# A paged MLA cache loop on one core: absorbed queries as extra columns of the key weights, keys in three banks, rope scores by page pairs

## The chip, the core and the metric

One core of a Trainium2 chip runs the whole kernel. TensorE (matrix products), VectorE, ScalarE and GpSimd each work through their own instructions in order; SyncE issues the DMAs. They wait for each other through semaphores. The metric is the time of one execution in microseconds, as the median of several runs.

## The reference, cut to what matters

The kernel computes one step of a decoder layer for 256 prompt tokens and for 8 sample sequences. The part that matters here is the attention of the samples over their cache. Each of the 8 sequences has 2048 past tokens, in 16 pages of 128; a page row holds a latent of 512 values and a rope key of 64. For each page, in the reference's words:

```python
def mla_keys(latent, w_uk, w_uv, k_norm_nope):
    c, kr = latent[..., :KV_LORA], latent[..., KV_LORA:]
    kn = rms_norm((c @ w_uk).reshape(bsz, s, MLA_HEADS, NOPE_DIM), k_norm_nope)
    v = (c @ w_uv).reshape(bsz, s, MLA_HEADS, V_DIM)
    return kn, kr, v

def mla_scores(qn, qr, kn, kr):
    s = jnp.einsum('bqhd,bkhd->bhqk', qn, kn) + jnp.einsum('bqhr,bkr->bhqk', qr, kr)
    return s.astype(jnp.float32) * MLA_SCALE
```

followed by a softmax over all tokens and a weighted sum of the values. The key of a token is divided by its root mean square in each head, so the full keys (`c @ w_uk`, 1024 columns, 8 heads of 128) have to be made for every cached token, if only for their squares. Beside this run the prompt's own attention, the gated-delta heads, and after the loop gates, merge and an MLP.

## The kernel before

**The loop.** The cache loop goes over `NT` = 128 pages, `n` = 0 to 127, in `NG` = 32 groups of four (`g = n // 4`, `t = n % 4`); one sample has four groups. There is no planner: every engine has its own loop over `n`, written out by hand, and the order in it is the order in which it works. Work of the rest of the layer is woven in as 256 slots, `beside(2 * n)` and `beside(2 * n + 1)`: prompt attention first (`front_pe` and the like), a few decay steps (`decay_steps`), then four pairs of gated-delta heads (`pair_pe`, `pair_act`, `pair_dve`), each of 49 slots.

**A page.** SyncE loads it into `clat` and `crope`, twelve pages at a time in a ring. VectorE separates its 16-bit halves (`split_planes`), a transposing DMA turns them, and ScalarE puts them together as `cTr` (`turned_page`), then rounds to the high part `cTh`. VectorE subtracts (`split_lo`) and gets the low part `cTl`. The key weights are in a high part `ukh` and a low part `ukl` as well, 1024 columns each. TensorE makes the keys in two halves of 512 columns (`keys(n, half_)`), each half in one of the banks 0 to 2 of PSUM, in 12 products: for each of four chunks of the latent `cTh` with `ukh`, `cTh` with `ukl` and `cTl` with `ukh` (lines 2016, 2017 and 2018). The page's latent is the stationary operand, loaded ahead of each product as 128 columns; the weights stream past it. ScalarE squares each half head by head out of PSUM and sums (`squares`, L851), into `kss`. Once a group is full, GpSimd raises its 32 columns to the power -1/2 (`rk`, L705).

**Scores.** The query of a head is folded through the key weights once ("absorbed", `qeff`), so that the scores need no finished keys, only `rk`. `qeff[:, s]` of sample `s` has 16 columns in each of five parts: columns 0 to 7 in parts 0 to 3 are the absorbed query, columns 8 to 15 in part 4 the rope part. Once in a group, at `t == 3`, `query_products` multiplies the latents of four pages (`cTr`, fp32, 512 moving columns, L2037) and the turned rope keys `rpT` (L2040) with it. The four chunks of the latent go to four strips of bank 4 and have to be added later. An fp32 product shows as two records, because it is done in two passes. ScalarE copies the bank to `prows` (`score_rows`, L862), TensorE turns it in four transposes a page later (`score_columns`, L2046), and VectorE adds the four strips (`score_parts`, L1240) to `sparts`. Then `scaled` multiplies by `rk` and adds the rope scores, `maxima` and `exps` make the softmax weights, and `weigh` (L2056) sums the page latents with them, a group and a page later. `rope_columns` (L2027) turns the rope keys of a group at `t == 2`, two pages in one transpose, and ScalarE copies them to `rpT` (`turned_rope`).

**Around it.** Before a bank is written again the key products wait for its squares: `wait(pe, "ksq_ready", k - 2)`, where `k` counts the halves and the bank is `k % 3`. After the last page come the column groups for gates and z (`z_unit`), which use banks 0 to 3.

Of the kernel before, what the change touches and what calls it, by code (L numbers as in the profile page):

```python
# [13 lines left out]
F32 = mybir.dt.float32  # L14
# [171 lines left out]
def build(nc, I, O):  # L186
    C_in, ctx = I["consts"], ExitStack()
    with ctx:
# [35 lines left out]
        qeff, e = place("qeff", [P, NS, 5, 16], F32, taken["rsq"][0])  # L224
# [5 lines left out]
        ukh, o = place("ukh", [P, 4, D], F32R, o)  # L230
        ukl, o = place("ukl", [P, 4, D], F32R, o)
# [97 lines left out]
        sparts, o = place("sparts", [P, 2, 4, 2, H], F32, o)  # L329
# [5 lines left out]
        gate, o = place("gate", [1, 1], F32, o)  # L335
        olat, _ = place("olat", [P, NS, 4, H], F32, taken["prows"][0])
# [123 lines left out]
        B_TR, B_SCORE, B_PAIR, B_ROWS = 3, 4, 5, 7  # L460
        trp = ps[:, B_TR, :].rearrange("p (c n) -> p c n", c=4)
        stp = ps[:, B_SCORE, :].rearrange("p (t n) -> p t n", t=4)

        def sum_bank(gg):

            return ps[:, 3 if gg < NG - 2 else 4, :]

        def latent_bank(s_):
            return sum_bank(4 * s_ + 3).rearrange("p (c n) -> p c n", c=4)

# [15 lines left out]
        def _(sp):  # L486
# [134 lines left out]
            sp.wait_ge(S("half_done"), 2 * NT)  # L621
            sp.wait_ge(S("qk_done"), NG)
# [52 lines left out]
        def _(g):  # L675
# [21 lines left out]
            nc.gpsimd.memset(qeff[:], 0.0).then_inc(S("pool_clear"), 1)  # L697
# [16 lines left out]
        def _(act):  # L714
# [116 lines left out]
            def turned_page(n):  # L831
# [3 lines left out]
                else:  # L835
                    act.wait_ge(S("tr_landed"), 16 * (n - 1))
                    if n % 4 == 0:
                        wait(act, "qk_done", n // 4)
                    nc.scalar.activation(cTr[:, :, tokens(n)].bitcast(U16).rearrange("p c (t x) -> p x c t", x=2), turned[:, n % 2].bitcast(U16).rearrange("p (x c t) -> p x c t", x=2, c=4), ACT.Copy).then_inc(S("ct_raw"), 1)  # L839
                act.wait_ge(S("ct_raw"), n + 1)  # L840
                wait(act, "half_done", 2 * (n - 1))
# [12 lines left out]
            def turned_rope(gg):  # L854
                act.wait_ge(S("rope_done"), gg + 1)
                wait(act, "qk_done", gg)
                nc.scalar.activation(rpT[:], ps[:, B_SCORE, 0:2 * P], ACT.Copy).then_inc(S("rope_ready"), 1)
# [140 lines left out]
            for n in range(NT):  # L998
# [5 lines left out]
                if t == 3:  # L1004
                    score_rows(g)
# [5 lines left out]
                squares(n, 1)  # L1011
            z_high(2)
# [72 lines left out]
        def _(v):  # L1085
# [147 lines left out]
            def split_lo(n):  # L1233
                v.wait_ge(S("ct_hi"), n + 1)
                wait(v, "half_done", 2 * (n - 1))
                V.tensor_tensor(cTl[:, n % 2], cTr[:, :, tokens(n)], cTh[:, n % 2].bitcast(F32), ALU.subtract).then_inc(S("ct_lo"), 1)  # L1236

            def score_parts(gg):
                v.wait_ge(S("st_done"), gg + 1)
                V.tensor_reduce(sparts[:, gg % 2].rearrange("p t a h -> p t (a h)"), stp.rearrange("p t (c n) -> p t n c", c=4)[:, :, 0:16, :], AX, ALU.add).then_inc(S("s_parts"), 1)  # L1240

            def scaled(gg):
                y = gg % 2
                v.wait_ge(S("s_parts"), gg + 1)
                v.wait_ge(S("rk_ready"), gg + 1)
                V.tensor_tensor(ssc[:, y], sparts[:, y, :, 0, :], rk[:, y], ALU.mult).then_inc(S("s_half"), 1)
                v.wait_ge(S("s_half"), gg + 1)
                V.tensor_tensor(ssc[:, y], sparts[:, y, :, 1, :], ssc[:, y], ALU.add).then_inc(S("s_ready"), 1)
# [55 lines left out]
            def front_dve(i):  # L1304
# [19 lines left out]
                if i == 4:  # L1324
                    v.wait_ge(S("pool_clear"), 2)
                    for g in range(2):
                        V.tensor_copy(qeff[:, :, 0:4, 4 * g:4 * g + 4], a_bank(f"qcol{g}").rearrange("p (c q x) -> p x c q", c=4, q=4)[:, 0:NS]).then_inc(S("a_read"), 1)
                    qx = qeff[:, :, 4, 8:16].rearrange("p s (a b) -> p a b s", b=2)
                    v.wait_ge(S("qrs_ready"), 1)
                    V.tensor_copy(qx[0:64, :, 0, :], qr[0:64, :, TP:T])  # L1330
                    V.tensor_copy(qx[64:128, :, 1, :], qr[64:128, :, TP:T])
                    v.wait_ge(S("qr64_landed"), 32)
                    V.tensor_copy(qx[0:64, :, 1, :], qr64[0:64])
                    V.tensor_copy(qx[64:128, :, 0, :], qr64[64:128]).then_inc(S("qeff_ready"), 1)
# [326 lines left out]
            for n in range(NT):  # L1661
# [4 lines left out]
                if t == 0 and g >= 1:  # L1666
                    score_parts(g - 1)
# [7 lines left out]
                if n == NT - 1:  # L1675
                    score_parts(g)
# [5 lines left out]
                if t == 3:  # L1682
                    v.wait_ge(S("ksq_ready"), 2 * n + 2)
# [172 lines left out]
        def _(pe):  # L1856
# [153 lines left out]
            def keys(n, half_):  # L2010
                k, cols = 2 * n + half_, slice(512 * half_, 512 * half_ + 512)
                out = ps[:, k % 3, :]
                pe.wait_ge(S("ct_lo"), n + 1)
                wait(pe, "ksq_ready", k - 2)
                for c in range(4):
# [3 lines left out]
                i.then_inc(S("half_done"), 1)  # L2019
# [513 lines left out]
```

## Time and profile before

| | us |
|---|---|
| median of 3 runs | 1457.36 |
| lowest and highest run | 1457.14, 1457.37 |
| span of the profiled execution (first to last instruction) | 1455.6 |
| TensorE busy | 1445.4 (99%) |
| ScalarE busy | 868.4 (60%) |
| VectorE busy | 808.5 (56%) |
| GpSimd busy | 217.1 (15%) |

The profile is of one execution, and its times count from its first instruction. It gives the span only; the runs are timed as a whole and have what lies around the span in them too. Durations of matrix products overlap, since they are pipelined: the time from one start to the next is what a product takes of the engine. A weight load has records of its own ("PEld"). A timeline joins neighbouring instructions of one line into one row with their number behind an x.

### The profile page before, as it was taken

What the parts mean: (1) busy time and instruction counts of PE and PEld (TensorE: products, weight loads), DVE (VectorE), ACT (ScalarE), POOL (GpSimd) and SP (SyncE); (2) the same over time, 40 slices, a digit from 0 to 9 for tenths busy, and PEclk for the clock granted to TensorE, in tenths of its full rate; (3) what the DMA queues carried; (4) which work ended last, traced back from release to release, by engine and by line L of the source; (5) the groups of instructions that cost most, each with busy time, mean ns of one, the idle gap of its engine ahead of it and who ended that gap; (6) DMA issues with size and microseconds to landing.
All of it is one profiled execution on the core that took longest, in us unless ns stands there. A gap on an engine that the chain in (4) does not pass through costs nothing.

```text
span 1455.6 us, 28542 instructions
## 1 busy us (share of the span) xinstructions
PE 1445.4 (99%) x10052; PEld 1182.0 (81%) x10052; DVE 808.5 (56%) x1664; ACT 868.4 (60%) x2816; POOL 217.1 (15%) x111
## 2 busy tenths in 40 slices
PE   9999999999999999999999999999999999999998
PEld 7877777877777777778777787777778999999998
DVE  5865445555546564555655555645434766777643
ACT  5545678686666686575855667766775353344332
POOL 3001111111122111111221111122122000000000
PEclk9999999999999999999999999999999999999999
DMA  9541315653245534365333453333734465555551
GB/s 280 172 119 30 83 26 117 156 116 70 63 102 123 121 86 86 74 132 125 85 70 82 113 139 70 63 70 73 189 77 152 145 235 183 168 172 191 181 174 59
DMA packets 263720, 173.61 MB, mean 119 GB/s; under 512 B 165464, under 2 KB 212088, under 8 KB 263576
## 3 DMA queue, kind: packets, MB, share of 16 engines
q1 hardware_dynamic: 263266, 171.53, 45.3%
q8 instruction: 78, 1.28, 0.4%
q14 instruction: 58, 0.48, 0.1%
q10 hardware_dynamic: 318, 0.33, 0.1%
HBM read 132.22 MB, written 6.74 MB: 95 GB/s over the span
## 4 chain that ended last, share of the span: by engine, by line
PE 96%; DVE 2%; ACT 0%; DMA 0%; ACTq 0%; issue 0%; POOL 0%; DVEq 0%
PE ps L2016 17%; PE ps L2018 16%; PE ps L2017 16%; PE ps L2453 6%; PE ps L2454 6%; PE ps L2455 6%; PE ps L2056 2%; PE ps L2037 2%; PE ps L2109 2%; PE ps L2401 2%; PE ps L2402 2%; PE ps L2110 2%; PE ps L2403 2%; PE ps L2111 2%; PE ps L1894 2%; PE ps L2046 1%
## 5 line engine op out<-in xcount | busy, mean ns | idle before, releaser
L851 ACT ACTIVATE ksq<-ps 128x128 f32<-128x128 f32 x1024 | 268.1, 277 | 279.5 <-PE ps L2018 278.0
L2016 PE MATMUL ps<-ukh,cTh 128*128 128x512 f32 x1024 | 418.4, 409 | 0.3 <-DVE cTl L1236 0.3
L2018 PE MATMUL ps<-ukh,cTl 128*128 128x512 f32 x1024 | 400.7, 391 | 0.0
L2017 PE MATMUL ps<-ukl,cTh 128*128 128x512 f32 x1024 | 399.9, 391 | 0.0
L705 POOL TENSOR_TENSOR rk<-kss,mhalf 128x32 f32<-128x32 f32 x32 | 180.1, 5628 | 478.0 <-DVE kss L1684 478.0
L2016 PEld LDWEIGHTS ps<-ukh,cTh 128*128 128x128 f32 x1024 | 192.6, 188 | 55.8 <-issue 17.1
L2018 PEld LDWEIGHTS ps<-ukh,cTl 128*128 128x128 f32 x1024 | 192.2, 188 | 42.9
L2017 PEld LDWEIGHTS ps<-ukl,cTh 128*128 128x128 f32 x1024 | 192.8, 188 | 34.0
L851 ACT ACTIVATION_READ_ACCUMULATOR ksq<-ps 128x1 f32 x1024 | 212.2, 207 | 0.0
L839 ACT ACTIVATE cTr<-turned 128x1024 uint16<-128x1024 uint16 x126 | 173.8, 1379 | 10.9 <-PE ps L2040 5.7
L1236 DVE TENSOR_TENSOR cTl<-cTr,cTh 128x512 fp32r<-128x512 f32 x128 | 88.4, 691 | 136.9 <-ACT cTh L842 136.0
L1038 ACT ACTIVATE wh<-wraw 128x2048 fp32r<-128x2048 f32 x44 | 84.3, 1916 | 131.3 <-PE ps L2455 126.8
L1688 DVE TENSOR_TENSOR wl<-wraw,wh 128x2048 fp32r<-128x2048 f32 x44 | 100.8, 2291 | 70.3 <-ACT wh L1038 70.3
L1231 DVE COPY planes<-clat 128x1024 uint16<-128x1024 uint16 x126 | 86.2, 684 | 21.8 <-DMA turned<-planes 14.6
L2453 PE MATMUL ps<-Ah,wh 128*128 128x264 f32 x320 | 91.1, 285 | 0.0
L2454 PE MATMUL ps<-Al,wh 128*128 128x264 f32 x320 | 90.9, 284 | 0.0
L2455 PE MATMUL ps<-Ah,wl 128*128 128x264 f32 x320 | 90.6, 283 | 0.0
L842 ACT ACTIVATE cTh<-cTr 128x512 fp32r<-128x512 f32 x128 | 80.9, 632 | 4.1
L2453 PE MATMUL ps<-Hh,wh 128*128 128x264 f32 x256 | 72.8, 284 | 0.0
L2455 PE MATMUL ps<-Hh,wl 128*128 128x264 f32 x256 | 72.7, 284 | 0.0
L2454 PE MATMUL ps<-Hl,wh 128*128 128x264 f32 x256 | 72.6, 284 | 0.0
L2453 PEld LDWEIGHTS ps<-Ah,wh 128*128 128x128 f32 x320 | 60.2, 188 | 0.0
(514 smaller groups left out, 2590.7 us busy)
## 6 DMA issues: line engine op xcount, KB each, us to landing
clat<-cache_mla SPq DMA_DIRECT2D x128, 256.0 KB, 2.6
wraw<-w_in SPq DMA_DIRECT2D x16, 1024.0 KB, 5.1
wraw<-w_up SPq DMA_DIRECT2D x16, 1024.0 KB, 5.4
wraw<-w_down SPq DMA_DIRECT2D x16, 1024.0 KB, 5.0
braw<-w_in SPq DMA_DIRECT2D x24, 512.0 KB, 4.0
crope<-cache_mla SPq DMA_DIRECT2D x128, 32.0 KB, 2.4
sst<-state_gdn SPq DMA_DIRECT2D x32, 128.0 KB, 3.2
gdn_sample<-sst SPq DMA_DIRECT2D x32, 128.0 KB, 2.0
```

The source lines that it names most:

```text
L705: nc.gpsimd.tensor_tensor(rk[:, y], kss[:, y], mhalf[:], ALU.pow).then_inc(S("rk_ready"), 1)
L839: nc.scalar.activation(cTr[:, :, tokens(n)].bitcast(U16).rearrange("p c (t x) -> p x c t", x=2), turned[:, n % 2].bitcast(U16).rearrange(" ...
L851: i = nc.scalar.activation(ksq[:, P * h:P * h + P], ps[:, k % 3, P * h:P * h + P], ACT.Square, accum_out=kss[:, n // 4 % 2, n % 4, 4 * hal ...
L1231: V.tensor_copy(planes[:].bitcast(U16).rearrange("p (x l) -> p x l", x=2), clat[:, n % RING, :].bitcast(U16).rearrange("p (l x) -> p x l", ...
L1236: V.tensor_tensor(cTl[:, n % 2], cTr[:, :, tokens(n)], cTh[:, n % 2].bitcast(F32), ALU.subtract).then_inc(S("ct_lo"), 1)
L1688: V.tensor_tensor(wl2[:, ns % 2], wraw2[:, (ns - NM) % 4], wh2[:, ns % 2].bitcast(F32), ALU.subtract).then_inc(S("w_lo"), 1)
L2016: mm(out, cTh[:, n % 2, c], ukh[:, c, cols], start=c == 0, stop=False)
L2017: mm(out, cTh[:, n % 2, c], ukl[:, c, cols], start=False, stop=False)
L2018: i = mm(out, cTl[:, n % 2, c], ukh[:, c, cols], start=False, stop=c == 3)
L2453: mm(out, w_hi, mh[:, kc, :], start=first and kc == 0, stop=False)
L2454: mm(out, w_hi, ml[:, kc, :], start=False, stop=False)
L2455: k = mm(out, w_lo, mh[:, kc, :], start=False, stop=last and kc == 3)
```

## The change

The absorbed query of the current sample is stored behind the key weights as columns 1024 to 1031, high part in `ukh`, low part in `ukl`. A page's keys are made in three banks: 384, 384 and 256 + 8 columns, with the same three kinds of product each. The last eight columns of the third bank are then the page's scores before scaling, already turned and summed over the chunks; ScalarE copies them to `sparts`. For every new sample (16 pages) VectorE copies that sample's columns into the weights (`query_slot`). The first four pages come before these columns are there; their scores are made once by `first_scores`. The rope scores of a group are two products with the turned rope keys as stationary operand, a pair of pages each, and 16 moving columns of `qrope`. `query_products`, `score_rows`, `score_columns` and `score_parts` are gone.

```diff
-        qeff, e = place("qeff", [P, NS, 5, 16], F32, taken["rsq"][0])
+        qeff, e = place("qeff", [P, NS, 4, H], F32, taken["rsq"][0])
+        qrope, e = place("qrope", [P, NS, 2 * H], F32, e)
+        qeffh, e = place("qeffh", [P, NS, 4, H], F32R, e)
-        ukh, o = place("ukh", [P, 4, D], F32R, o)
-        ukl, o = place("ukl", [P, 4, D], F32R, o)
+        ukh, o = place("ukh", [P, 4, D + H], F32R, o)
+        ukl, o = place("ukl", [P, 4, D + H], F32R, o)
+        KG = [(slice(0, 384), 0, 3, False), (slice(384, 768), 3, 3, False), (slice(768, 1024), 6, 2, True)]
...
-            def squares(n, half_):
-                k = 2 * n + half_
-                act.wait_ge(S("half_done"), k + 1)
-                if half_ == 0 and n % 4 == 0:
+            def squares(n, j):
+                k, (_, h0, count, scored) = 3 * n + j, KG[j]
+                act.wait_ge(S("group_done"), k + 1)
+                if j == 0 and n % 4 == 0:
                     wait(act, "rk_ready", n // 4 - 1)
+                    wait(act, "s_half", n // 4 - 1)
                 wait(act, "ksq_ready", k)
-                for h in range(4):
-                    i = nc.scalar.activation(ksq[:, P * h:P * h + P], ps[:, k % 3, P * h:P * h + P], ACT.Square, accum_out=kss[:, n // 4 % 2, n % 4, 4 * half_ + h:4 * half_ + h + 1])
+                if scored and n >= 4:
+                    nc.scalar.activation(sparts[:, n // 4 % 2, n % 4, :], ps[:, k % 3, P * count:P * count + H], ACT.Copy)
+                for h in range(count):
+                    i = nc.scalar.activation(ksq[:, P * h:P * h + P], ps[:, k % 3, P * h:P * h + P], ACT.Square, accum_out=kss[:, n // 4 % 2, n % 4, h0 + h:h0 + h + 1])
                 i.then_inc(S("ksq_ready"), 1)
...
-            def score_rows(gg):
-                act.wait_ge(S("qk_done"), gg + 1)
-                wait(act, "st_done", gg)
-                nc.scalar.activation(prows[:], ps[:, B_SCORE, :], ACT.Copy).then_inc(S("ssb_ready"), 1)
...
-                if t == 3:
-                    score_rows(g)
...
                 squares(n, 1)
+                squares(n, 2)
...
-            def score_parts(gg):
-                v.wait_ge(S("st_done"), gg + 1)
-                V.tensor_reduce(sparts[:, gg % 2].rearrange("p t a h -> p t (a h)"), stp.rearrange("p t (c n) -> p t n c", c=4)[:, :, 0:16, :], AX, ALU.add).then_inc(S("s_parts"), 1)
+            def query_slot(s_):
+                wait(v, "group_done", 48 * s_)
+                V.tensor_copy(ukh[:, :, D:D + H], qeffh[:, s_])
+                V.tensor_copy(ukl[:, :, D:D + H], qeffl[:, s_]).then_inc(S("slot_ready"), 1)
...
+                v.wait_ge(S("rope_scored"), gg + 1)
+                V.tensor_tensor(ssc[:, y], rope_scores_of(gg), ssc[:, y], ALU.add).then_inc(S("s_ready"), 1)
...
+                    V.tensor_copy(qeffh[:], qeff[:]).then_inc(S("qeff_ready"), 1)
+                    v.wait_ge(S("qeff_ready"), 1)
+                    V.tensor_tensor(qeffl[:], qeff[:], qeffh[:].bitcast(F32), ALU.subtract).then_inc(S("qeff_split"), 1)
...
                 if n + 1 < NT:
                     split_lo(n + 1)
-                if t == 0 and g >= 1:
-                    score_parts(g - 1)
+                if n and n % 16 == 0:
+                    query_slot(n // 16)
...
-            def keys(n, half_):
...
+            def key_chunks(n, j, chunks):
+                k, (cols, _, count, scored) = 3 * n + j, KG[j]
+                if scored and n >= 4:
+                    cols = slice(cols.start, cols.stop + H)
+                    pe.wait_ge(S("slot_ready"), n // 16 + 1)
+                out = ps[:, k % 3, 0:cols.stop - cols.start]
+                if chunks[0] == 0:
+                    pe.wait_ge(S("ct_lo"), n + 1)
+                    wait(pe, "ksq_ready", k - 2)
+                for c in chunks:
...
-                wait(pe, "s_parts", gg)
+                wait(pe, "s_ready", gg)
...
-            def query_products(gg):
...
-                for c in range(4):
-                    mm(ps[32 * c:32 * c + 16, B_SCORE, :], qeff[:, s, c, :], cTr[:, c, :], start=True, stop=False)
...
+            def rope_scores(gg):
+                pe.wait_ge(S("rope_ready"), gg + 1)
+                pe.wait_ge(S("qeff_ready"), 1)
+                for m in range(2):
+                    out = rope_scores_of(gg)[:, 2 * m:2 * m + 2, :].rearrange("p t h -> p (t h)")
+                    k = mm(out, rpT[:, P * m:P * m + P], qrope[:, gg // 4, :], start=True, stop=True)
+                k.then_inc(S("rope_scored"), 1)
+
+            def first_scores():
+                pe.wait_ge(S("ct_raw"), 4)
+                pe.wait_ge(S("qeff_ready"), 1)
                 for t in range(4):
+                    for c in range(4):
+                        k = mm(ps[:, B_ROPE, 384 + H * t:384 + H * t + H], cTr[:, c, tokens(t)], qeff[:, 0, c, :], start=c == 0, stop=c == 3)
...
                 if t == 3:
-                    query_products(g)
+                    rope_scores(g)
+                if n == 3:
+                    first_scores()
...
-                if t == 0 and g >= 1:
-                    score_columns(g - 1)
...
                 beside(2 * n)
-                keys(n, 0)
+                key_chunks(n, 0, (0, 1, 2, 3))
+                key_chunks(n, 1, (0,))
...
                 beside(2 * n + 1)
-                keys(n, 1)
+                key_chunks(n, 1, (1, 2, 3))
+                key_chunks(n, 2, (0, 1, 2, 3))
```

`group_done` counts the three groups of a page where `half_done` counted two halves, and every wait on it is scaled to that. The last two groups' weighing uses bank 7 instead of bank 4, and `z_unit` goes through the banks in the order 3, 0, 1, 2 instead of 3, 1, 2, 0.

## Rows read from the trace of the kernel before

**Rows 1.** Busy time by stretch: the cache loop (us, busy us and instructions of each engine, clock, DMA).
```profile
101.00:1112.80 1011.80, 1011.34 (x6592) 765.37 (x6593) 526.07 (x1386) 681.50 (x2632) 195.60 (x93) 1.00 0.42 94
```

**Rows 2.** Waits in the cache loop, TensorE and ScalarE (us in total, times, longest).
```profile
PE ps L2016 <- DVE cTl L1236: 0.3, 1, 0.3
...
ACT ksq L851 <- PE ps L2018: 276.1, 193, 3.4
```

**Rows 3.** Groups by form, ScalarE: table loads (xcount, busy us, mean ns).
```profile
L870 ACT ACT_TABLE_LOAD x10 | 12.8, 1283 | 0.2
```

**Rows 4.** Timeline of TensorE (start us, duration): 512 columns, quiet and behind other work.
```profile
242.12 0.39 PE L2016 MATMUL ps<-ukh,cTh 128*128 128x512 f32 x1
...
244.62 0.39 PE L2018 MATMUL ps<-ukh,cTl 128*128 128x512 f32 x1
...
710.10 0.40 PE L2017 MATMUL ps<-ukl,cTh 128*128 128x512 f32 x1
...
712.41 0.39 PE L2018 MATMUL ps<-ukh,cTl 128*128 128x512 f32 x1
```

**Rows 5.** Timeline of TensorE: first and last of 36 products of 264 columns.
```profile
1249.73 0.28 PE L2453 MATMUL ps<-Bh,wh 128*128 128x264 f32 x1
...
1253.98 0.29 PE L2455 MATMUL ps<-Bh,wl 128*128 128x264 f32 x1
```

**Rows 6.** Timeline of TensorE's weight loads in that stretch.
```profile
1249.85 0.19 PEld L2455 LDWEIGHTS ps<-Bh,wl 128*128 128x128 f32 x1
1249.97 0.19 PEld L2453 LDWEIGHTS ps<-Bh,wh 128*128 128x128 f32 x1
```

**Rows 7.** Timeline of TensorE around query blocks, alone and before others.
```profile
231.72 0.39 PE L2018 MATMUL ps<-ukh,cTl 128*128 128x512 f32 x1
...
233.35 0.50 PE L2016 MATMUL ps<-ukh,cTh 128*128 128x512 f32 x1
...
555.50 0.39 PE L2018 MATMUL ps<-ukh,cTl 128*128 128x512 f32 x1
...
557.52 0.50 PE L2016 MATMUL ps<-ukh,cTh 128*128 128x512 f32 x1
...
352.24 0.39 PE L2018 MATMUL ps<-ukh,cTl 128*128 128x512 f32 x1
...
352.94 0.50 PE L2016 MATMUL ps<-ukh,cTh 128*128 128x512 f32 x1
```

**Rows 8.** Timeline of TensorE around the score transposes.
```profile
238.72 0.40 PE L2018 MATMUL ps<-ukh,cTl 128*128 128x512 f32 x1
...
239.32 0.48 PE L2016 MATMUL ps<-ukh,cTh 128*128 128x512 f32 x1
239.63 0.39 PE L2017 MATMUL ps<-ukl,cTh 128*128 128x512 f32 x1
```

**Rows 9.** Timeline of TensorE around eight records with 8 columns.
```profile
103.95 0.95 PE L2282 MATMUL ps<-qr,consts_sb 128*128 128x8 f32 x8
104.76 0.48 PE L2016 MATMUL ps<-ukh,cTh 128*128 128x512 f32 x1
```

**Rows 10.** Timeline of ScalarE on pages 15 and 16.
```profile
235.49 0.58 ACT L862 ACTIVATE prows<-ps 128x512 f32<-128x512 f32 x1
...
242.38 0.25 ACT L851 ACTIVATE ksq<-ps 128x128 f32<-128x128 f32 x1
...
243.38 1.34 ACT L839 ACTIVATE cTr<-turned 128x1024 uint16<-128x1024 uint16 x1
```

**Rows 11.** Timelines of VectorE and TensorE on page 48.
```profile
505.69 0.68 DVE L1236 TENSOR_TENSOR cTl<-cTr,cTh 128x512 fp32r<-128x512 f32 x1
...
506.09 0.50 PE L2016 MATMUL ps<-ukh,cTh 128*128 128x512 f32 x1
```

**Rows 12.** Timelines of VectorE and TensorE at page 17.
```profile
245.41 0.69 DVE L1236 TENSOR_TENSOR cTl<-cTr,cTh 128x512 fp32r<-128x512 f32 x1 [1.73 <-ACT cTh L842]
...
246.19 0.50 PE L2016 MATMUL ps<-ukh,cTh 128*128 128x512 f32 x1
```

More of the change, by code:

```diff
@@ L328, in build @@
         prows, o = place("prows", [P, 512], F32, o)
-        sparts, o = place("sparts", [P, 2, 4, 2, H], F32, o)
+        sparts, o = place("sparts", [P, 2, 4, H], F32, o)
         lacc, o = place("lacc", [P, 512], F32, o)
@@ L335, in build @@
         gate, o = place("gate", [1, 1], F32, o)
+        qeffl, _ = place("qeffl", [P, NS, 4, H], F32R, taken["prows"][0])
         olat, _ = place("olat", [P, NS, 4, H], F32, taken["prows"][0])
@@ L855, in turned_rope @@
                 act.wait_ge(S("rope_done"), gg + 1)
-                wait(act, "qk_done", gg)
-                nc.scalar.activation(rpT[:], ps[:, B_SCORE, 0:2 * P], ACT.Copy).then_inc(S("rope_ready"), 1)
-            def score_rows(gg):
-                act.wait_ge(S("qk_done"), gg + 1)
-                wait(act, "st_done", gg)
-                nc.scalar.activation(prows[:], ps[:, B_SCORE, :], ACT.Copy).then_inc(S("ssb_ready"), 1)
+                wait(act, "rope_scored", gg)
+                nc.scalar.activation(rpT[:], ps[:, B_ROPE, 0:2 * P], ACT.Copy).then_inc(S("rope_ready"), 1)
             def exps(gg):
@@ L1234, in split_lo, with first_parts @@
                 v.wait_ge(S("ct_hi"), n + 1)
[L1235 removed]
+                wait(v, "group_done", 3 * (n - 1))
                 V.tensor_tensor(cTl[:, n % 2], cTr[:, :, tokens(n)], cTh[:, n % 2].bitcast(F32), ALU.subtract).then_inc(S("ct_lo"), 1)
[L1238 to L1240 removed]
+            def first_parts():
+                v.wait_ge(S("first_scores"), 1)
+                V.tensor_copy(sparts[:, 0], ps[:, B_ROPE, 384:416].rearrange("p (t h) -> p t h", h=H)).then_inc(S("first_parts"), 1)
+            def query_slot(s_):
+                wait(v, "group_done", 48 * s_)
+                V.tensor_copy(ukh[:, :, D:D + H], qeffh[:, s_])
+                V.tensor_copy(ukl[:, :, D:D + H], qeffl[:, s_]).then_inc(S("slot_ready"), 1)
             def scaled(gg):
                 y = gg % 2
[L1244 removed]
+                if gg == 0:
+                    v.wait_ge(S("first_parts"), 1)
                 v.wait_ge(S("rk_ready"), gg + 1)
[L1246 removed]
+                V.tensor_tensor(ssc[:, y], sparts[:, y], rk[:, y], ALU.mult).then_inc(S("s_half"), 1)
                 v.wait_ge(S("s_half"), gg + 1)
[L1248 removed]
+                v.wait_ge(S("rope_scored"), gg + 1)
+                V.tensor_tensor(ssc[:, y], rope_scores_of(gg), ssc[:, y], ALU.add).then_inc(S("s_ready"), 1)
             def maxima(gg):
@@ L2018, in keys @@
                     i = mm(out, cTl[:, n % 2, c], ukh[:, c, cols], start=False, stop=c == 3)
-                i.then_inc(S("half_done"), 1)
+                if chunks[-1] == 3:
+                    i.then_inc(S("group_done"), 1)
             def rope_columns(gg):
@@ L2023, in rope_columns @@
                     pe.wait_ge(S(f"page_landed{u % RING}"), 32 * (u // RING) + 32)
-                wait(pe, "s_parts", gg)
+                wait(pe, "s_ready", gg)
                 for m in range(2):
                     u = (4 * gg + 2 * m) % RING
-                    k = nc.tensor.transpose(ps[:, B_SCORE, P * m:P * m + P], crope[:, u:u + 2, :].rearrange("p u n -> p (u n)"), ident)
+                    k = nc.tensor.transpose(ps[:, B_ROPE, P * m:P * m + P], crope[:, u:u + 2, :].rearrange("p u n -> p (u n)"), ident)
                 k.then_inc(S("rope_done"), 1)
-            def query_products(gg):
-                s = gg // 4
-                pe.wait_ge(S("ct_raw"), 4 * gg + 4)
+            def rope_scores(gg):
                 pe.wait_ge(S("rope_ready"), gg + 1)
                 pe.wait_ge(S("qeff_ready"), 1)
-                wait(pe, "s_parts", gg)
-                for c in range(4):
-                    mm(ps[32 * c:32 * c + 16, B_SCORE, :], qeff[:, s, c, :], cTr[:, c, :], start=True, stop=False)
-                for t in range(4):
-                    r = slice(64 * (t % 2), 64 * (t % 2) + 64)
-                    k = mm(ps[32 * t:32 * t + 16, B_SCORE, P * t:P * t + P], qeff[r, s, 4, :], rpT[r, P * (t // 2):P * (t // 2) + P], start=False, stop=True)
-                k.then_inc(S("qk_done"), 1)
-            def score_columns(gg):
-                pe.wait_ge(S("ssb_ready"), gg + 1)
-                for t in range(4):
-                    k = nc.tensor.transpose(stp[:, t, :], prows[:, P * t:P * t + P], ident)
-                k.then_inc(S("st_done"), 1)
+                for m in range(2):
[5 more added lines that the diff above has]
+                pe.wait_ge(S("qeff_ready"), 1)
+                for t in range(4):
+                    for c in range(4):
+                        k = mm(ps[:, B_ROPE, 384 + H * t:384 + H * t + H], cTr[:, c, tokens(t)], qeff[:, 0, c, :], start=c == 0, stop=c == 3)
+                k.then_inc(S("first_scores"), 1)
             def weigh(gg):
@@ L2390, in z_unit @@
                 pe.wait_ge(S("w_lo"), ns + 1)
-                for j in ((3, 1, 2, 0) if i == 0 else range(4)):
+                for j in ((3, 0, 1, 2) if i == 0 else range(4)):
                     if i == 0 and j == 3:
@@ L2394, in z_unit @@
                     elif i == 0:
-                        pe.wait_ge(S("ksq_ready"), max(k + 1 for k in range(2 * NT) if k % 3 == j))
+                        pe.wait_ge(S("ksq_ready"), 3 * (NT - 1) + j + 1)
                     if i >= 2 and i % 2 == 0:
```

47 lines of the change are left out of this document (22 added, 25 removed).

## The prediction

> **What bounds the kernel now.** I read the stretches first. The cache loop runs from 101 to 1112.8 us, 1011.8 of the 1455.6 us; TensorE is busy for 1011.34 of it at a granted clock of 1.00, which is the 2.4 GHz level, while VectorE has 526 us of work and ScalarE 682 [rows 1]. Busy time of a pipelined engine proves little, so I read the waits next: in the loop the key products wait once, for 0.3 us, and ScalarE spends 276 us waiting for them [rows 2]. So TensorE's instruction stream sets the pace in every part of the loop, and an edit is worth what it adds to that stream or takes from it, until another engine comes late. The third view is therefore the timeline of TensorE, read from start to start, because durations overlap there: a 512-column product lasts 0.39 us but the next starts after 0.23.
>
> Start to start: in a quiet stretch 11 products of 512 columns take 2.50 us, 0.227 each; behind other work 10 take 2.31 us, 0.231 [rows 4]. I use 0.229. Products of 264 columns: 35 steps in 4.25 us, 0.1214 each [rows 5]. At 2.4 GHz the columns alone are 0.2133 and 0.1100 us, so a product costs its columns and a further 0.0157 us (512) or 0.0114 us (264).
>
> **Part 1: keys in three banks.** A page had 24 products of 512 columns; it gets 24 of 384 and 12 of 264 (256 on the first four pages). No row has 384 columns. Its bounds are columns plus the one or the other surcharge, 0.1714 and 0.1757; between two measured sizes I take the middle, 0.1736. Then a page costs 24 x 0.1736 + 12 x 0.1214 = 5.62 us against 24 x 0.229 = 5.50: +0.127 us, times 128 = **+16.3 us**. With the small surcharge throughout it is +9.6, with the large one in all 36 products +29.4. These are the ends.
>
> The Trainium skill ("TensorE: Matmul & The Clock Gate", Back-to-back issue gap) gives a warm product columns / 2.4 GHz and about 2.5 ns. By that rule the estimate for this part would be 9 us instead of 16. The trace does not agree at either size (0.227 and 0.1214 us where the rule has 0.216 and 0.1125), so the rows decide.
>
> **Part 2: query products go, rope scores come.** Alone in its place, the block of old query and rope products stretches the way from the last key product to the next from 0.23 to 1.63 us: 1.40. In front of a block of small products the way is 2.02 us, with that block alone 0.70: 1.32 [rows 7]. There are 32 blocks, one for each group of four pages. The new rope scores are two fp32 products, four records, each behind a load of 128 columns. The nearest row is eight records of this kind with 8 moving columns: 0.81 us from their start to the next key product's, 0.10 to 0.11 each [rows 9]. Four add 0.37 alone and 0.45 before others. Eight groups stand alone and save 1.03, 24 save 0.87: **-29.1 us**, with ends -28 and -33. The first key behind such a block has a longer step (0.34 instead of 0.23) before and after the change; it stays.
>
> **Part 3: score transposes go.** Four a group: the way is 0.60 us instead of 0.23, and the next step 0.31 instead of 0.23 [rows 8], together 0.45; 0.44 where others follow. 32 times: **-14.1 us**.
>
> **Part 4: the first page group.** 16 products with loads of 128 columns and 8 moving columns, in two passes 32 records at 0.11 [rows 9]: **+3.6 us**, once, on TensorE's own stream. The transposes of rope stay as they are.
>
> **Part 5: the other engines.** ScalarE loses 32 row copies of 0.58 us, 18.6 us, and gains 124 copies of 8 columns, each at most the 0.25 of a square over 128 columns [rows 10], so at most 31 us. VectorE loses a reduction a group and gains two small copies for each of eight samples, and at the front a split of the query columns. GpSimd's power step gets its sums somewhat earlier, and the sum with the rope scores is read a page before the next rope transposes want that bank. All of it is covered by the 330 us and 486 us in which these engines have nothing to do in the loop [rows 1]; without that cover it would be at most some 10 us. After the last key product of a page ScalarE has now one small copy and two squares to make instead of four before it turns the next page, about 0.3 us less. So the next page's operands come a little earlier.
>
> **Part 6: new waits.** There are now as many groups a page as banks, so each page needs the same bank again: from a group's end to its reuse some 3.5 us of key products, where it was 5.5. And the third group of every 16th page waits for VectorE to put in the new query columns, which stands in its queue behind the split of the next page. Seven such pages. On six it is covered; the latest split is on page 48: it ends at 506.37 and with the two copies, some 0.2 us each, at about 506.8, while the second half of the keys starts at 506.09 [rows 11], and the third group starts 1.4 us behind that point (24 products of 384 columns before it instead of 12 of 512), at 507.5. On page 16 it isn't covered. There ScalarE goes through several table loads (decays, exponentials): the squares of page 15's second half start only at 242.38, and page 17 is turned from 243.38 on [rows 10], split at 245.41, and page 17's keys start at 246.19, with nothing to spare [rows 12]. In the new order: without the row copy (0.58), with one square fewer ahead (0.25) and 0.35 from page 14, the squares start at about 241.2 and are done at 242. The keys of page 15 and 16 come 1.3 us earlier (the two blocks above), so page 16 begins at 238.05 and wants bank 1 at 240.1: it waits 2.0 us. The second group ends at 244.2; the split, 0.6 earlier than before, ends at 245.4, the two copies at 245.9: another 1.7 us. Queued behind that waiting product are the rest of page 16, the weighing of page values and page 17; nothing after them makes it up. **+3.7 us**, from 0 to 6. Page 116, where a late transposing DMA leaves small room, adds **0.3**.
>
> **Sum.** +16.3 - 29.1 - 14.1 + 3.6 + 3.7 + 0.3 = -19.3 us. The profiled span is 1455.6; the median of the runs is 1457.36, 1.8 us more for what lies around the span and does not change. 1457.4 - 19.3 = **1438 us**. Of 1457 us, 0.2% is 2.9 us, about what a measurement of this kernel can tell from no change.
>
> **Rivals.**
> *The surcharge does not shrink with the columns* (0.0157 in all 36). For it: it is larger in the 512-column rows behind other work. Against it: 0.0114 at 264. 1438 + 13 = 1451 us. Chance 0.12.
> *The surcharge is the small one, and page 16 waits less.* 1438 - 6.7 - 3.7 = about 1428 us. Chance 0.12.
> *Banks come free late, slower than before.* The mechanism: a table load of ScalarE (1.28 us) ahead of squares holds a bank that the next page now needs 2 us sooner. The loop has some 26 such places besides page 16, ten before exponentials [rows 3] and, by the code, four each for silu, exp and two roots. If each held TensorE for its 1.28 us, it would cost 33 us: 1471. It outweighs the gain from 0.74 us a place. Against it: ScalarE waits for key products 193 times in the loop [rows 2], so it is mostly early; page 16 has three table loads in 6 us, the others one or two. Chance 0.08.
> *Weight loads become the bound.* A page has 36 loads instead of 24, each 0.19 us. If no product could follow sooner than a load takes, a page would need 36 x 0.188 = 6.8 us, +146 us over the forecast: 1584. Against it: in the later stages loads of 0.19 us start every 0.12 us [rows 6], so they overlap. Chance 0.01.
> The Trainium skill ("Perfetto Trace Analysis", Identifying the Most-Contended Engine) asks to judge TensorE by the busy share of its loads, which speaks against this change: it rises. Here the stretch with 264 columns has loads without a gap [rows 6] and still runs at columns plus 0.011 us, so the share names no bound.
> *The change frees nothing.* Another chain (pages by DMA, turning, splitting) is just as long as TensorE's, and what is saved comes back as waits: 1457. Against it: 276 us of ScalarE's waiting. Chance 0.05.
> The forecast keeps 0.62, with its own range 1431 to 1446.
>
> **Chances and range.** Both surcharge cases end faster than 1454.4, so faster has 0.62 + 0.12 + 0.12 = 0.86, and 0.01 of the last rival's milder forms: 0.87. Same 0.05. Slower 0.08 (the 1471 and the load bound, less that 0.01). The range takes in the forecast and most of the two surcharge cases: 1430 to 1450.
>
> **What would show it.** Key products of 384 columns starting every 0.172 to 0.175 us, of 264 every 0.121 to 0.123; no records with 16-column weights over 512 moving columns, nor of the score transposes; four records of rope scores a group within 0.45 us; 32 short records once near 124 us. Near page 16 TensorE standing still twice, for some 2 us each, behind squares and behind the copies into the key weights. The loop shorter by 19 us, the rest after it unchanged. It is wrong if the step of 384 columns is above 0.18, or if waits for squares show in many pages.

## The result and the profile after

The changed kernel takes 1442.04 us (median of 4 runs, 1440.28 to 1442.27) against 1457.36; the ratio is 0.9888, 95% interval 0.9877 to 0.9900. That is 15.3 us less where 19.3 were forecast, inside the stated range. The profiled execution has a span of 1440.5 us. The stretches first, loop and rest (columns as in [rows 1]):

```profile
102.90:1098.20 995.30, 992.02 (x7650) 923.31 (x7651) 517.59 (x1372) 686.30 (x2727) 197.99 (x93) 1.00 0.43 96
1098.20:1440.50 342.30, 338.19 (x2817) 334.57 (x2816) 214.28 (x203) 132.43 (x107) 6.12 (x3) 1.00 0.52 170
```

From the first key product to the last it is 995.1 us, before 1011.8 [rows 1]: 16.7 less. The rest after the loop is the same within 0.2. The stage ahead of the loop, which the change hardly touches, took 1.8 us more in this profile; more on that below. TensorE has 1058 more records in the loop and still sets the pace; its loads now show 923 us of 995, and no wait in the loop names a load.

The waits in the loop, for TensorE and for ScalarE (us in total, times, longest):

```profile
PE ps L2035 <- ACT ksq L859: 1.5, 1, 1.5
PE ps L2035 <- DVE ukl L1247: 1.2, 1, 1.2
PE ps L2100 <- DVE qkv L1511: 0.5, 1, 0.5
PE ps L2035 <- DVE cTl L1238: 0.3, 1, 0.3
```

```profile
ACT ksq L859 <- PE ps L2037: 182.4, 157, 3.0
```

The first two lines are the two waits that the prediction put on page 16, each once in 128 pages. ScalarE still waits far more for TensorE than the other way round. The timeline of TensorE shows where they lie (L2035 to L2037 are the three kinds of key product):

```profile
244.65 0.34 PE L2037 MATMUL ps<-ukh,cTl 128*128 128x384 f32 x1
246.45 0.41 PE L2035 MATMUL ps<-ukh,cTh 128*128 128x384 f32 x1 [1.47 <-ACT ksq L859]
...
248.46 0.34 PE L2037 MATMUL ps<-ukh,cTl 128*128 128x384 f32 x1
249.97 0.39 PE L2035 MATMUL ps<-ukh,cTh 128*128 128x264 f32 x1 [1.16 <-DVE ukl L1247]
```

Page 16's second group stands for page 15's squares, its third for the query columns of the second sample.

Now the step of the new widths, on page 124, where little other work runs. First rows of the two widths and the last of the page:

```profile
1077.60 0.34 PE L2037 MATMUL ps<-ukh,cTl 128*128 128x384 f32 x1
...
1079.13 0.28 PE L2037 MATMUL ps<-ukh,cTl 128*128 128x264 f32 x1
```

From 1077.60, the last of 384 columns, there are 12 steps to 1079.13. The first of them is the step of a 384-column product, the other eleven are of 264 columns: 1.53 - 0.175 = 1.35, 0.123 each. Over the whole loop, record to record, without waits and without the few steps in which the clock was at its lower level (below), 2749 steps of 384 columns inside a run of key products have a mean of 0.1754 us and 1372 steps of 264 have 0.1216; the 2622 steps of 512 before had 0.2289. With the steps at the lower clock in it the mean for 384 is 0.1758, so such means of two kernels can be compared only when both leave them out. The prediction took 0.1736, 0.1214 and 0.229.

The rope scores and the first scores, in the same timeline:

```profile
126.34 0.52 PE L2055 MATMUL ps<-qrope,rpT 128*128 128x16 f32 x4
126.70 3.72 PE L2063 MATMUL ps<-qeff,cTr 128*128 128x8 f32 x32
130.28 1.10 PE L2324 MATMUL ps<-qr,consts_sb 128*128 128x256 f32 x2
130.82 0.88 PE L2035 MATMUL ps<-ukh,cTh 128*128 128x384 f32 x1
131.50 0.52 PE L2036 MATMUL ps<-ukl,cTh 128*128 128x384 f32 x1
```

The block of 32 short records takes 3.6 us, as forecast. The products behind it were not forecast: 0.52 us long instead of 0.34 and 0.32 from start to start instead of 0.175. The stretches there show why (the third number from the end is the granted clock):

```profile
126.00:130.00 4.00, 4.00 (x39) 4.00 (x37) 0.00 (x0) 0.63 (x5) 0.00 (x0) 1.00 0.28 53
130.00:134.00 4.00, 4.00 (x16) 3.82 (x16) 1.82 (x4) 2.00 (x2) 0.00 (x0) 0.57 0.00 0
134.00:138.00 4.00, 4.00 (x27) 3.95 (x26) 1.79 (x4) 1.66 (x12) 0.00 (x0) 1.00 0.00 0
```

The clock is at its lower level, 1.2 GHz, for 3.4 us right behind the block, although TensorE was never idle in it.

The loop's balance, in the prediction's parts (sums of steps from start to start over all records of the loop):

| | forecast | measured |
|---|---|---|
| keys, steps and seams | +16.3 | +21.1 (754.1 - 730.3 - 2.7 of waits) |
| query products against rope scores | -29.1 | -29.6 (42.3 to 12.6) |
| score transposes | -14.1 | -13.4 |
| first scores | +3.6 | +3.6 |
| waits on page 16 | +3.7 | +2.7 |
| page 116, others | +0.3 | -1.1 |
| loop | -19.3 | -16.7 |

The lower clock is inside these numbers, mostly in the keys' row; an experiment prices it at 1.6.

### The profile page after: what moved, and what is told of

Its sections match the earlier page's. It is cut to its first block, busy times and chain, and to the rows that moved or that the text cites. A ratio compares the mean times of both kernels' runs of the same rounds, so it can differ in the third digit from the quotient of the medians.

```text
span 1440.5 us, 30928 instructions
## 1 busy us (share of the span) xinstructions
PE 1427.6 (99%) x11108; PEld 1340.9 (93%) x11108; DVE 800.0 (56%) x1651; ACT 872.6 (61%) x2908; POOL 219.4 (15%) x111
## 4 chain that ended last, share of the span: by engine, by line
PE 95%; ACT 2%; DVE 2%; issue 0%; POOL 0%; DVEq 0%; ACTq 0%
PE ps L2035 17%; PE ps L2036 16%; PE ps L2037 16%; PE ps L2470 6%; PE ps L2471 6%; PE ps L2472 6%; PE ps L2073 2%; PE ps L2126 2%; PE ps L2418 2%; PE ps L2419 2%; PE ps L2127 2%; PE ps L2420 2%; PE ps L2128 2%; PE ps L1909 1%; PE ps L2055 1%; PE ps L2100 1%
## 5 line engine op out<-in xcount | busy, mean ns | idle before, releaser
L2035 PE MATMUL ps<-ukh,cTh 128*128 128x384 f32 (+1 forms) x1536 | 507.4, 330 | 2.9 <-ACT ksq L859 1.5
L2036 PE MATMUL ps<-ukl,cTh 128*128 128x384 f32 (+1 forms) x1536 | 491.9, 320 | 0.0
L2037 PE MATMUL ps<-ukh,cTl 128*128 128x384 f32 (+1 forms) x1536 | 491.4, 320 | 0.0
L2035 PEld LDWEIGHTS ps<-ukh,cTh 128*128 128x128 f32 x1536 | 289.8, 189 | 24.3 <-issue 17.6
L2036 PEld LDWEIGHTS ps<-ukl,cTh 128*128 128x128 f32 x1536 | 289.5, 188 | 0.8
L2037 PEld LDWEIGHTS ps<-ukh,cTl 128*128 128x128 f32 x1536 | 288.9, 188 | 0.0
L859 ACT ACTIVATION_READ_ACCUMULATOR ksq<-ps 128x1 f32 x1024 | 209.2, 204 | 0.0
L2471 PEld LDWEIGHTS ps<-Al,wh 128*128 128x128 f32 x320 | 60.2, 188 | 0.0
```

The costliest lines, as they stand in the source:

```text
L2035: mm(out, cTh[:, n % 2, c], ukh[:, c, cols], start=c == 0, stop=False)
L2036: mm(out, cTh[:, n % 2, c], ukl[:, c, cols], start=False, stop=False)
L2037: i = mm(out, cTl[:, n % 2, c], ukh[:, c, cols], start=False, stop=c == 3)
L2471: mm(out, w_hi, ml[:, kc, :], start=False, stop=False)
```

## The experiments

All comparisons of a few us are made by the length of the loop, first to last key product, in the profiles. Steps are means over the loop at the upper clock, without waits. Two profiles of the unaltered changed kernel gave 995.13 and 995.14 us. The medians of the runs move by 2 us with the stage ahead of it.

### Three banks alone

The kernel before, with nothing of the change but the three groups of key columns:

```diff
...
+        KG = [(slice(0, 384), 0, 3), (slice(384, 768), 3, 3), (slice(768, 1024), 6, 2)]
...
-                keys(n, 0)
+                key_chunks(n, 0, (0, 1, 2, 3))
+                key_chunks(n, 1, (0,))
...
-                keys(n, 1)
+                key_chunks(n, 1, (1, 2, 3))
+                key_chunks(n, 2, (0, 1, 2, 3))
...
```

> The kernel before with one part of the change alone: keys in banks of 384, 384 and 256 columns, no score columns; query products and score transposes stay. Theory (the three banks cost 24 x 0.1758 + 12 x 0.118 - 24 x 0.2289 = 0.14 us a page, 18 us in all, some 3 less at the seams, and a wait for squares on page 16 of 1 to 3 us): 1457.4 + 17 = 1474 us, from 1472 to 1478. Rival (reusing each bank on every page makes waits in many pages): above 1485, with waits of key products for squares in many pages. Rival (the banks cost what the surcharge of 0.0136 said): 1457.4 + 11 = 1468.

1473.74 us (ratio to before 1.0110, 1.0093 to 1.0127), the loop 1027.9, 16.1 more than before. Its waits:

```profile
PE ps L2019 <- ACT ksq L852: 1.4, 1, 1.4
PE ps L2019 <- DVE cTl L1238: 0.3, 1, 0.3
```

So the reuse of a bank on every page costs one wait of 1.4 us, not one in many pages. The other 14.7 us are the smaller products, and both rivals are out. One number did not fit: its 384-column steps have a mean of 0.1744 us, where the changed kernel has 0.1754.

### The first scores in four parts

```diff
...
-                if n == 3:
-                    first_scores()
+                if n in (3, 4):
+                    first_scores(2 * (n - 3))
...
+                if n in (3, 4):
+                    first_scores(2 * (n - 3) + 1)
                 beside(2 * n + 1)
...
```

(the parts left out make one score block of one page per call and fit the waits on it)

> The changed kernel with the 32 records of the first scores not in one block, but eight at a time between four blocks of key products (pages 3 and 4). Theory (the block of 32 records with 8 moving columns is what the clock falls behind, to the lower level for 3.4 us, which costs about 1.9 us): no fall between 120 and 145 us in the profile, 1442.0 - 1.9 = 1440.1 us. Rival (the fall comes at any place, as the one at 52 us does where the change has no part): a fall in the loop still, or the time unchanged at 1442.

1438.61 us, the loop 993.5: 1.6 less. The stretch that had the fall, in this kernel:

```profile
124.00:128.00 4.00, 4.00 (x27) 3.95 (x27) 1.87 (x4) 2.77 (x8) 0.00 (x0) 1.00 0.10 19
128.00:132.00 4.00, 4.00 (x30) 3.95 (x29) 1.79 (x4) 1.45 (x12) 0.00 (x0) 1.00 0.00 0
```

The same 32 records, eight at a time between key products, and the clock stays up. In the three kernels with the parts spread, this one and the two joined ones, no profile has a fall in the loop. Nor have the profiles of the kernel before and of the three banks alone, which make no first scores. In all eight profiles of kernels with the block in one piece there is one, and it begins between 127.8 and 130.9 us, from within the block's last records to 1.3 us behind it. The theory holds and the rival doesn't. What it is in the block that brings the fall was not taken apart.

### Query columns ahead of the split

```diff
...
+                if n and n % 16 == 0:
+                    query_slot(n // 16)
                 if n + 1 < NT:
                     split_lo(n + 1)
-                if n and n % 16 == 0:
-                    query_slot(n // 16)
```

> The changed kernel with VectorE putting in the next sample's query columns ahead of the split of the next page instead of behind it. Theory (the second wait on page 16, 1.2 us, is for the place in VectorE's queue): this wait is gone and the time is 1442.0 - 1.2 = 1440.8 us. Rival (page 17 is late anyway, since ScalarE turns it late): the wait moves to page 17's first product, time unchanged.

1440.14 us, the loop 993.7: 1.4 less. The wait for `ukl` is gone and no other came in its place. It was the place in VectorE's queue: two copies of 0.17 us each stood behind a split that waits for ScalarE.

### The sigmoid a page later as well

```diff
-                if i == 2:
+                if i == 4:
                     act.wait_ge(S("rw_clear"), 1)
```

(and the order of the run before)

> The changed kernel with the query columns put in ahead of the split (as in the run before) and the decays' sigmoid, with its table load, moved one page later on ScalarE. Theory (the first wait on page 16, 1.5 us, is for squares that stand behind three table loads in 6 us): that wait is gone too, the loop 993.7 - 1.5 = 992.2 us. Rival (the work is only pushed to page 17, where ScalarE is the later for it): a wait of about the same length on page 17 or 18, the loop unchanged at 993.7.

1440.32 us, the loop 993.3. The wait for squares is gone, but the rival was right:

```profile
PE ps L2378 <- issue: 1.3, 1, 1.3
```

L2378 is the transpose of the decays on page 17, which needs the sigmoid. The wait went from 1.5 to 1.3 us and otherwise only changed its name.

### The same columns as 512, 256 and 264

```diff
-        KG = [(slice(0, 384), 0, 3, False), (slice(384, 768), 3, 3, False), (slice(768, 1024), 6, 2, True)]
+        KG = [(slice(0, 512), 0, 4, False), (slice(512, 768), 4, 2, False), (slice(768, 1024), 6, 2, True)]
...
```

> The changed kernel with the same 1032 columns and the same 36 products a page, split as 512, 256 and 264. Theory (the surcharge over the columns is 0.0156 us for 512 and 384 and 0.008 to 0.012 for 256 and 264, so the loss of part 1 is the width 384): a page costs 12 x (0.2289 + 0.1179 + 0.1217) = 5.62 instead of 5.68 us, 128 pages 7.5 us less: 1434.5 us. Rival (the surcharge is one per product, whatever the width): 1442. Rival (four squares hold the first bank longer than three and the key products wait for it): 256-column steps as in the theory, but waits for squares in several pages and a time of 1438 or more.

1439.85 us, the loop 993.2, 1.9 less; the forecast of 7.5 was wrong. 256 and 264 columns have their steps (0.1186, 0.1211), but 512 columns now take 0.2303 where they took 0.2289 in the kernel before. By these steps a page is 5.64 us against 5.67, 3.8 us in 128 pages. So it isn't the width 384. Here too the wide steps became longer than in the kernel before, and in both kernels the rows of the key weights lie 1032 columns apart instead of 1024. The rest of the difference is a second fall of the clock, 3.4 us long, at 248 us behind the two waits on page 16; at the 1.6 us that the other fall cost it hides nearly half of the gain. The waits are two and 2.7 us in all, as in the changed kernel, so the rival of the four squares is out too.

### The distance of the rows

Only the memory that the key weights take is changed. With it everything placed behind them moves:

```diff
-        ukh, o = place("ukh", [P, 4, D + H], F32R, o)
-        ukl, o = place("ukl", [P, 4, D + H], F32R, o)
+        ukh, o = place("ukh", [P, 4, 1088], F32R, o)
+        ukl, o = place("ukl", [P, 4, 1088], F32R, o)
```

> The changed kernel with the rows of the key weights 1088 columns apart in memory (4352 bytes, a multiple of 256) instead of 1032 (4128 bytes, a multiple of 32); nothing else differs. Theory (the 384-column steps are 0.1758 here and 0.1744 with rows of 1024 columns because of the distance of the rows): steps of 0.1744, 24 x 0.0014 x 128 = 4.3 us less. Rival (the steps are longer because of what the other engines do at that time): steps unchanged at 0.1758, time unchanged.

1436.78 us (ratio to before 0.9847), the loop 990.1: **5.0 us less**, with every wait where it was. Page 124 in this kernel:

```profile
1072.01 0.33 PE L2036 MATMUL ps<-ukl,cTh 128*128 128x384 f32 x1
...
1073.56 0.28 PE L2036 MATMUL ps<-ukl,cTh 128*128 128x264 f32 x1
```

The row at 1072.01 is the second last product of 384 columns, the one at 1073.56 the second last of 264. Between them are 12 steps in 1.55 us. Two of them are steps of 384 columns, together 0.35; the ten of 264 columns share 1.20, 0.120 each. Over the loop the means are 0.1743 for 384 and 0.1199 for 264, against 0.1754 and 0.1216. That is some 3 us in the steps of 384 columns and 2 in those of 264. The expected 4.3 us came from the wide steps alone, at 0.0014 each, a difference that had some of the lower clock in it; they gained 0.0011, and the steps of 264 columns, which the expectation left out, made up for it. The step that it named, 0.1744, is right, and the rival is out.

> As the run with 1088 columns, with rows 1040 columns apart (4160 bytes, a multiple of 64 and not of 128). If the row distance matters by multiples of 64 bytes, steps of 384 columns are 0.1744; if it takes a larger power of two, 0.1758 as with 1032.

1439.24 us (two runs), the loop 994.9. The steps of 384 columns are 0.1751, those of 264 columns 0.1208: both lie between the two other distances, 384 columns nearer to the bad one. The loop hides it, because the fall of the clock lasts twice as long in this profile, 6.8 us:

```profile
126.00:128.00 2.00, 2.00 (x19) 2.00 (x19) 0.00 (x0) 0.00 (x0) 0.00 (x0) 0.95 0.03 8
128.00:130.00 2.00, 2.00 (x9) 1.89 (x9) 0.00 (x0) 0.68 (x1) 0.00 (x0) 0.50 0.00 0
132.00:134.00 2.00, 2.00 (x8) 2.00 (x8) 0.13 (x1) 0.00 (x0) 0.00 (x0) 0.50 0.00 0
```

With the second half of the fall taken off at another 1.6 us, an estimate from the run with the first scores spread, the loop would be 993.3: 1.8 us less than with 1032, where 1088 gives 5.0. So neither branch of the expectation fits: a distance of 4160 bytes, a multiple of 64 and not of 128, is a little better than 4128 and not good. 4096 and 4352, multiples of 256, are. Whether 128 would do was not tried.

At 4160 bytes `ukl` and all that lies behind it start at the same place within 256 bytes as at 4096 and 4352; at 4128 `ukl` alone starts 128 bytes off. So where a tensor starts within 256 bytes does not explain the slow steps at 4160, and the distance of the rows is left. That the tensors also lie at other addresses altogether was not varied by itself.

### Four groups a page

The same as 256, 256, 256 and 264 columns, 48 products a page:

```diff
...
+        KG = [(slice(0, 256), 0, 2, False), (slice(256, 512), 2, 2, False), (slice(512, 768), 4, 2, False), (slice(768, 1024), 6, 2, True)]
...
+                key_chunks(n, 1, (0, 1, 2, 3))
...
+                key_chunks(n, 3, (0, 1, 2, 3))
...
```

> The changed kernel with the 1032 columns in four groups a page: 256, 256, 256 and 264, so 48 products instead of 36. Theory (a product's surcharge grows with its width, 0.012 at 256, 0.0154 at 384): steps of 0.1185 us, a page 36 x 0.1185 + 12 x 0.1217 = 5.73 us, only 0.05 more than with 36 products, 6 us in all, besides waits for banks, since three banks serve four groups. Rival (the surcharge is one for every product that adds): 12 x 0.0154 = 0.18 us a page more, 24 us. Rival (weight loads become the bound): steps of 256 columns well above 0.12 us.

1454.30 us, the loop 1008.4, 13.2 more. Its waits for squares:

```profile
PE ps L2036 <- ACT ksq L859: 7.6, 10, 1.5
```

The waits for squares are 6.1 us more than in the changed kernel, the wait for `ukl` (1.2) is gone, and the products themselves add some 8: 12 more on each of 128 pages, at steps of 0.1185 us for 256 columns. The theory had this step right and 6 us for the products. The rival's 24 is out, and so are the weight loads as a bound at this width. Four groups over three banks show what a bank that comes free late looks like: ten waits instead of one.

### Joined, and the changed kernel once more

```diff
...
-                if t == 3 and g >= 1:
-                    exps(g - 1)
                 beside(2 * n + 1)
                 squares(n, 1)
                 squares(n, 2)
+                if t == 3 and g >= 1:
+                    exps(g - 1)
...
```

(with rows 1088 apart, the first scores in four parts and the query columns ahead of the split)

> The changed kernel with rows of the key weights 1088 columns apart, first scores in four parts, query columns ahead of the split, and on every fourth page ScalarE's exponentials behind the page's last squares instead of between them. Theory (the four add up: 5.0 for the row distance and 1.6 for the clock and 1.4 for the second wait, all as measured alone, and up to 1.5 for the first wait): the loop 995.1 - 9.5 = 985.6 us, the time about 1432. Rival (the exponentials only move page 17 back, as the sigmoid did): the loop 987.1 and a wait on page 17.

**1432.22 us** (1430.48 to 1432.75; ratio to before 0.9823, 0.9809 to 0.9836), the fastest version, with the loop at 985.5 us where 985.6 was expected. What is left at this place is 1.0 us:

```profile
PE ps L2035 <- ACT ksq L859: 1.0, 1, 1.0
PE ps L2022 <- ACT cTr L839: 0.8, 1, 0.8
```

The first line is now page 17's first key product: most of the first wait moved there, as with the sigmoid. (The second line lies ahead of the loop.) That the sum came out to 0.1 us is in part luck. Compared page by page with the run with 1088 columns, the loop is 1.6 us shorter on pages 3 and 4 (the clock) and 2.0 on page 16, where 2.9 were expected: the exponentials gave 0.6 and not 1.5. Another 0.9 us is saved on page 76, where the wait on L2100 (0.6 us in that run) is gone; the expectation had no term for it. Why it went stays open.

> The same with the columns split as 512, 256 and 264. Theory (with rows 1088 apart the steps are 0.229, 0.118 and 0.120, a page 5.60 us instead of 5.635): 4 us less than the joined one with 384. Rival (what 512 saves, it loses in the waits for four squares): within 1 us of the joined one.

1432.62 us, the loop 985.9: no gain. The 512-column steps are back at 0.2292 with this row distance, but those of 256 and 264 columns are 0.1192 and 0.1205, not 0.118 and 0.120, and with 384 columns they are 0.1743 and 0.1199. By these steps a page takes 5.63 us against 5.62: there was nothing to save. The wait at page 17, 1.5 us instead of 1.0, is the rest. The rival had the number right and the reason mostly wrong.

> The changed kernel once more, unaltered, beside the joined ones. Theory (single runs lie in two groups 2 us apart by whether the clock falls for 3.4 us in the stage before the loop): runs near 1440.2 and near 1442.1, none between 1440.8 and 1441.6; and a profile has its first key product at 102 to 103 us with such a fall and at 100 to 101 without.

1440.72 us, runs at 1439.55, 1440.43, 1441.00 and 1442.39. The loop repeats to 0.01 us, the stage ahead of it doesn't: this profile has its first key product at 101.6 us and no fall at 52, the first one had it at 102.9 with the clock down for 3.4 us there (stretches from the first profile, then from this one):

```profile
52.00:56.00 4.00, 4.00 (x23) 4.00 (x22) 3.27 (x5) 0.81 (x2) 0.00 (x0) 0.59 0.40 146
```

```profile
52.00:56.00 4.00, 4.00 (x34) 3.97 (x33) 3.11 (x5) 1.21 (x3) 0.00 (x0) 1.00 0.48 171
```

That is 23 products in four us against 34, the same program. The runs don't fall in two clear groups as I expected, since one lies at 1441.0, and the first key product is at neither 102 to 103 nor 100 to 101 us; the clock at the very start varies too, with a lower stretch of 3.4 us in the first profile and 6.8 in this one. The runs of the kernel before spread in the same way, from 1456.6 to 1459.6. Its median beside this run was 1457.68, which makes the difference 17.0 us here against 15.3 in the result.

## Why the prediction held, and what it had wrong

**What bounds the kernel: right.** TensorE's stream set the pace everywhere, in all the profiles of changed kernels. ScalarE's 124 extra copies took 0.18 us each, 22 us where the prediction had at most 31; outside of page 16 no wait of the key products names ScalarE.

**Parts 2 to 4: right, each to 0.7 us.** -29.6, -13.4 and +3.6 against -29.1, -14.1 and +3.6. The eight-column record [rows 9] was a good price for both new kinds of product.

**Part 1: the right mechanism, the term too small.** "Between two measured sizes I take the middle, 0.1736": it was 0.1754, a surcharge of 0.0154 and so nearly the large one, while 264 columns kept nearly the small one (0.1216). It is above the 0.172 to 0.175 that the prediction named as its sign. The steps make +22.4 us where +16.3 was forecast, the lower clock another 1.4, and the steps between key products and other work, for which the prediction had no term, gave 2.7 back: +21.1. The runs took the miss of 0.0018 apart. With rows 1024 apart the step is 0.1744, so the middle was off by 0.0008. The other 0.0010 is the distance of the rows, 1032 columns: the diff shows it, and the prediction did not ask what it does to the products. Padding them takes 5.0 us off the loop, of which about 3 are in the steps of 384 columns; the step of 264 was priced from rows that had 0.1214 already.

**The first scores: right in themselves, with a cost behind them that was missed.** The clock falls behind the block; spreading the block took 1.6 us off the loop.

**Part 6: right in place and kind.** Two waits, on page 16, for squares behind table loads and for query columns behind a split: 1.5 and 1.2 us against 2.0 and 1.7. The other six samples and page 116 cost nothing. One small wait of 0.5 us on a gated-delta step was not foreseen.

**The rivals.** Late banks in many places: out, one wait in 128 pages here and ten with four groups. Weight loads as the bound: out, 923 of 995 us of the loop show a load, and the steps do not lengthen with it. The Trainium skill ("Perfetto Trace Analysis", Identifying the Most-Contended Engine) judges TensorE's headroom by MFU, the share of the peak arithmetic rate, and by the busy share of the loads. Here the share of time in which a load runs rose from 76% to 93% of the loop, and stands at 98% behind it, where 264 columns still take 0.121 us a step; so in this trace the share of the loads by itself showed no limit. The constant surcharge: out for 264 columns (0.0116); for 384 it comes near by its size (0.0154), but more than half of what lies above the middle is from the distance of the rows. That nothing would be freed: out.

The sum: of the 4.0 us between 19.3 and 15.3, 2.6 lie in the loop, -16.7 instead of -19.3. The keys are 4.8 dearer (steps 6.1 and clock 1.4, less 2.7 at the seams to other work), the waits 1.0 and all the rest 1.2 cheaper. So the forecast is nearer than its parts: what was dearer than forecast comes to 8.2 us, and 5.6 us that it did not foresee, or had too dear, made up for it. That is luck. The other 1.4 lie around the loop, where the clock ahead of it differs from run to run.

## What to carry to other kernels

Where TensorE's stream is the bound, count start-to-start steps at each width and keep the width dependence: here a product costs its columns and 11 to 16 ns, so putting eight columns into existing products is cheap even at half as many products again. When an operand grows by a few columns, look at the distance of its rows too, and pad it if steps get longer. When a bank or an operand slot is asked for once in a while, look for the one page where its maker is latest; and a fix that moves work on the late engine tends to move the wait with it.

## What the runs showed of the hardware that was not expected

- With the rows of the moving operand 4128 bytes apart, products of 384 columns took 0.1754 us each from start to start, with 4160 bytes 0.1751, with 4096 and 4352 bytes 0.1744 and 0.1743. For 264 columns it was 0.1216, 0.1208 and, at 4352 bytes, 0.1199; for 512 columns 0.2303 at 4128 against 0.2289 and 0.2292. Steps of 256 columns show no such loss: 0.1186 at 4128, 0.1188 at 4096, 0.1192 at 4352. What in the memory does it was not found.
- The clock fell to its lower level, 1.2 GHz, for 3.4 us (once 6.8) at the end of or behind 3.6 us of short products (128-column loads, 8 moving columns), in eight of eight profiles, though TensorE's records leave no gap in them. The Trainium skill ("TensorE: Matmul & The Clock Gate", HAM oscillation) ties falls to idle gaps; here the engine was busy by the profile, and spreading the same records kept the clock up in three of three.
- At 264 columns and 98% of the time in loads (334.57 of 342.30 us after the loop), a product still costs its columns and 11 ns (0.1213 us in the mean), though a load lasts 0.19.
